# Moving the normed rows by 16 bytes relative to the streamed weights

## Chip, core and metric

The kernel runs on one core of one Trainium2 chip. The metric is the device time of one execution in microseconds, the median of several executions. TensorE (PE) multiplies, VectorE (DVE), ScalarE (ACT) and GpSimd (POOL) work elementwise, SyncE (SP) issues the weight transfers. PEld is the engine's load of stationary operands, which overlaps the matmul before.

## The reference

256 tokens (T) of width 1024 (D = 8 chunks of 128) pass through four layers in fp32. Two layers have a mixer, a memory cross attention and a product-key expert layer with 16384 experts; two have a mixer and a gated feed-forward layer of width 2816. Every sublayer begins with a norm and ends with an addition to h:

```python
def rmsnorm(x, g):
    y = x * lax.rsqrt(jnp.mean(x * x, axis=-1, keepdims=True) + EPS)
    return y * g

for l in range(DEPTH):                              # first block
    h = h + mixer[l](rmsnorm(h, mix_norm[l]))
    h = h + memory_cross_attn(rmsnorm(h, xattn_norm[l]), mem_n, ...)
    h = h + peer_ffn(rmsnorm(h, peer_norm[l]), ...) # gelu(x . u[e]) weights the rows v[e]
h = rmsnorm(h, final_norm)
for l in range(DEPTH):                              # second block
    h = h + mixer2[l](rmsnorm(h, attn_norm_2[l]))
    gate, up = split(rmsnorm(h, ffn_norm_2[l]) @ f_w_gate_up_2[l])
    h = h + (silu(gate) * up) @ f_w_down_2[l]
return rmsnorm(h, final_norm_2)
```

The expert layer multiplies the normed rows with all 16384 rows of peer_u and the weighted result with all of peer_v.

## The kernel before

Everything lies feature on partition: h and the normed rows are tiles of 128 partitions by 8 chunks by 256 tokens. Each fp32 number that enters a weight product is split into a high part, rounded to fp32r, and a low part, the rest: the normed rows into hnH and hnL, a weight block of 128x1024 into wH and wL. `product` makes one product out of three fp32r matmuls (L796 to L798 in the profile):

```python
pe.matmul(dst, lh, rh, start=start, stop=False, skip_group_check=True)  # weights high, rows high
pe.matmul(dst, lh, rl, start=False, stop=False, skip_group_check=True)  # weights high, rows low
pe.matmul(dst, ll, rh, start=False, stop=stop, skip_group_check=True)   # weights low, rows high
```

The second argument is the stationary operand (128x128, loaded ahead of its matmul), the third the moving one. The profile names the moving operand first: `bank<-hnH,wH` streams 256 columns of hnH past a 128x128 piece of wH.

The weights come as 864 blocks in the order of use, two at a time (1 MB) by SP (L660), into two ring slots. ACT copies a block to wH (L540), DVE or for some blocks POOL subtracts to wL (L551); there are four buffers of each. A buffer comes free when PE is done with its block.

The stages use `product` in these ways:

- `lin` (all linear layers, and `ffn` for gate and up): per output tile 8 chunks of 3 matmuls, the normed rows moving, 24 matmuls a block. `lin` also takes other moving tiles that are split in the same way: memH/memL, att_OTH/att_OTL, ycatH/ycatL, od_yH/od_yL, pr_hH/pr_hL, od_hH/od_hL, and ff_aH/ff_aL in the down layer.
- `acts` in `peer`: the same with a block of 128 experts, 128 blocks a layer. For 64 of them `tokens` follows each block with four 128x128 matmuls of one-hot rows (L1016).
- `outs` in `peer`: wH and wL are the moving operand (512 columns), wgtH/wgtL the stationary one, 12 matmuls a block.
- `token_major`: wH and wL moving (512 or 128 columns), memH or hnH stationary.

Every engine's instructions stand in the order in which the code is written; semaphores tie them together, and nothing is scheduled by the compiler.

Tiles are laid into the on-chip memory one behind the other in the order of their `sb` calls, and nothing else sets their addresses. Bytes from the start of a partition: arena 16512, ring 147584, wH 163968, wL 180352, the tile named shared (wgtH, wgtL) behind it, small 204928, snk, then hnH 205376 and hnL 213568, act_out 221760, vec, con 224352, iww, rb, slotT 226176. Modulo 256, wH and wL begin at 128 and hnH and hnL at 64: the rows begin 64 bytes below the weights. The other moving tiles of `lin` lie in the arena at the same remainder of 64 (gaps such as `od_gap` and `pr_gap` put them there); wgtH and wgtL have the weights' remainder of 128. All pieces that a weight product streams (1024 bytes of a chunk) or loads (512 bytes of a weight block) begin at those remainders; only in the few products of width 96, whose pieces have 384 bytes, every second one begins 128 bytes further.

Of the kernel before, what the change touches and what calls it, by code (L numbers as in the profile page):

```python
# [18 lines left out]
P = 128  # L19
T = 256  # L20
NT = T // P
D = 1024
DC = D // P
# [19 lines left out]
F32R = mybir.dt.float32r  # L43
# [272 lines left out]
def build_stacks(nc, x, mem, vecs, cst, w_stream, iw_w, sinks, rel_bias, c_cnt, c_neg, c_masks, c_bucket,  # L316
# [25 lines left out]
    with ExitStack() as ctx:  # L342
        def sb(name, shape, dt=F32):
            return ctx.enter_context(nc.sbuf_tensor(name, shape, dt))
# [4 lines left out]
        def stage(*wanted):  # L349

            with ExitStack() as scope:
                held = [scope.enter_context(nc.sbuf_tensor(name, [P] + list(shape), dt)) for name, shape, dt in wanted]
                return [t[tuple([slice(None)] * (len(w[1]) + 1))] for t, w in zip(held, wanted)]


        AR = 32768 - DC * T
        h = stage(("h_before", [AR], F32), ("h", [DC, T], F32))[1]
        (gates,) = stage(("gates", [N_KEYS, T], F32))
        h_back, sums = stage(("h_back", [DC, T], F32), ("sums", [NT, D], F32))

        MEM0, ATT0 = AR - 2 * DC * T - 16, AR - 2 * DC * T - 9344
        _, memH, memL = stage(("mem_before", [MEM0], F32), ("memH", [DC, T], F32R), ("memL", [DC, T], F32R))
# [68 lines left out]
        small = sb("small", [P, 96])  # L431
        snk = sb("snk", [P, 16])

        hnH, hnL = sb("hnH", [P, DC, T], F32R), sb("hnL", [P, DC, T], F32R)
        act_out = sb("act_out", [P, 2, T])
        root_sb, mem_root = act_out[:, 0, :], act_out[:, 1, :]
        vec = sb("vec", [P, NVEC])
        con = sb("con", [P, NCST])
        iww = sb("iww", [P, DC, 8])
        rb = sb("rb", [32, 8])  # L440
        slotT = sb("slotT", [P, 3, T])
        eps = small[:, 80:81]
        lbv = sb("lbv", [P, 24])
# [2160 lines left out]
```

## Time and profile before

| | us |
|---|---|
| median of 3 executions | 2812.21 (2805.3 to 2812.48) |
| profiled execution, its own time | 2813.5 |
| its span in the trace, first to last instruction | 2811.2 |
| PE busy | 2714.5 |
| DVE busy | 2053.1 |
| ACT busy | 1454.5 |
| mean granted TensorE clock | 0.99 |

The profiled execution stands 1.3 us above the median, and 2.3 us of it lie outside the span. A matmul's record overlaps that of its neighbours, since the ends are modelled; the time that one costs in a row of them is the distance between two starts. A row of the view by windows gives the matmuls that touch a stretch, the two or three that had begun before it among them.

### The profile page before, as it was taken

What the parts mean: (1) busy time and instruction counts of PE and PEld (TensorE: products, weight loads), DVE (VectorE), ACT (ScalarE), POOL (GpSimd) and SP (SyncE); (2) the same over time, 40 slices, a digit from 0 to 9 for tenths busy, and PEclk for the clock granted to TensorE, in tenths of its full rate; (3) what the DMA queues carried; (4) which work ended last, traced back from release to release, by engine and by line L of the source; (5) the groups of instructions that cost most, each with busy time, mean ns of one, the idle gap of its engine ahead of it and who ended that gap; (6) DMA issues with size and microseconds to landing.
All of it is one profiled execution on the core that took longest, in us unless ns stands there. A gap on an engine that the chain in (4) does not pass through costs nothing.

```text
span 2811.2 us, 57248 instructions
## 1 busy us (share of the span) xinstructions
PE 2714.5 (97%) x19552; PEld 2544.1 (90%) x19552; DVE 2053.1 (73%) x4430; ACT 1454.5 (52%) x2378; POOL 177.8 (6%) x141
## 2 busy tenths in 40 slices
PE   7999999999999999989999999999999989999998
PEld 6999899999988888979998999988888889999998
DVE  8557997886566667876699888567776877666665
ACT  5455345444555555555544444455555565446544
POOL 0004000000000000000374000000000100000000
PEclk9999999999999999999999999999999999999999
DMA  5445566455766665424456555676666525563454
GB/s 190 176 157 184 204 215 213 174 182 195 261 242 242 242 242 179 149 78 165 165 182 217 191 172 183 218 258 242 242 242 242 187 81 182 190 230 117 177 184 178
DMA packets 140451, 546.19 MB, mean 194 GB/s; under 512 B 15784, under 2 KB 81592, under 8 KB 83616
## 3 DMA queue, kind: packets, MB, share of 16 engines
q1 hardware_dynamic: 63216, 455.38, 44.8%
q10 hardware_dynamic: 73728, 67.14, 7.4%
q0 software_dynamic: 3376, 21.88, 2.0%
q8 instruction: 87, 1.43, 0.2%
q14 instruction: 44, 0.36, 0.0%
HBM read 505.53 MB, written 40.91 MB: 194 GB/s over the span
## 4 chain that ended last, share of the span: by engine, by line
PE 78%; DVE 15%; DMA 2%; ACT 2%; issue 2%; DVEq 0%; ACTq 0%; SPq 0%
PE bank L796 23%; PE bank L797 23%; PE bank L798 23%; PE bank L1016 4%; DVE wL L551 4%; DMA ring<-in_w_stream 2%; PE bank L917 1%; ACT wH L540 1%; PE bank L937 1%; DVE pr_eq L1969 1%; DVE pr_eq L1971 1%; DVE pr_m L1973 1%; PE bank L928 1%; DVE pr_m L1924 0%; DVE pr_i L1924 0%
## 5 line engine op out<-in xcount | busy, mean ns | idle before, releaser
L551 DVE TENSOR_TENSOR wL<-ring,wH 128x1024 fp32r<-128x1024 f32 x809 | 988.1, 1224 | 605.5 <-ACT wH L540 602.5
L540 ACT ACTIVATE wH<-ring 128x1024 fp32r<-128x1024 f32 x864 | 907.3, 1055 | 423.2 <-DMA ring<-in_w_stream 252.6
L796 PE MATMUL bank<-hnH,wH 128*128 128x256 f32 x3528 | 1003.3, 284 | 34.5 <-DVE wL L551 26.6
L797 PE MATMUL bank<-hnL,wH 128*128 128x256 f32 x3528 | 984.0, 279 | 0.0
L798 PE MATMUL bank<-hnH,wL 128*128 128x256 f32 x3528 | 983.5, 279 | 0.0
L796 PEld LDWEIGHTS bank<-hnH,wH 128*128 128x128 f32 x3528 | 667.5, 189 | 45.7 <-issue 22.9
L797 PEld LDWEIGHTS bank<-hnL,wH 128*128 128x128 f32 x3528 | 667.2, 189 | 0.5 <-issue 0.2
L798 PEld LDWEIGHTS bank<-hnH,wL 128*128 128x128 f32 x3528 | 665.1, 189 | 0.0
L796 PE MATMUL bank<-wH,wgtH 128*128 128x512 f32 x1024 | 398.5, 389 | 0.3 <-DVE wgtL L2010 0.3
L798 PE MATMUL bank<-wH,wgtL 128*128 128x512 f32 x1024 | 398.4, 389 | 0.0
L797 PE MATMUL bank<-wL,wgtH 128*128 128x512 f32 x1024 | 398.3, 389 | 0.0
L1478 ACT ACTIVATE act_out<-bank 128x256 f32<-128x256 f32 x256 | 97.6, 381 | 339.0 <-PE bank L798 280.1
L1502 ACT ACTIVATE wgtH<-gates 128x256 fp32r (+1 forms) x256 | 106.9, 418 | 252.1 <-PE bank L798 251.9
L796 PEld LDWEIGHTS bank<-wH,wgtH 128*128 128x128 f32 x1024 | 192.2, 188 | 40.6 <-issue 0.7
L798 PEld LDWEIGHTS bank<-wH,wgtL 128*128 128x128 f32 x1024 | 192.2, 188 | 39.9
L797 PEld LDWEIGHTS bank<-wL,wgtH 128*128 128x128 f32 x1024 | 192.2, 188 | 39.7
L1997 DVE TENSOR_SCALAR onehot<-con,slotT 128x128 f32<-128x128 f32 x512 | 174.1, 340 | 0.0
L551 POOL TENSOR_TENSOR wL<-ring,wH 128x1024 fp32r<-128x1024 f32 x55 | 141.8, 2598 | 68.9 <-DVE wL L551 41.2
L1996 DVE TENSOR_SCALAR onehot<-con,slotT 128x128 f32<-128x128 f32 x512 | 143.1, 280 | 0.0
L1016 PE MATMUL bank<-onehot 128*128 128x128 f32 x1024 | 134.9, 274 | 0.0
L1016 PEld LDWEIGHTS bank<-onehot 128*128 128x128 f32 x1024 | 124.8, 191 | 0.0
L2010 DVE TENSOR_TENSOR wgtL<-gates,wgtH 128x256 fp32r<-128x256 f32 x256 | 107.6, 420 | 8.8 <-ACT wgtH L1502 8.4
(411 smaller groups left out, 3535.3 us busy)
## 6 DMA issues: line engine op xcount, KB each, us to landing
ring<-in_w_stream SPq DMA_DIRECT2D x432, 1024.0 KB, 4.9
act_parked<-act_out ACTq DMA_DIRECT2D x256, 128.0 KB, 3.0
act_in<-act_parked ACTq DMA_DIRECT2D x256, 128.0 KB, 2.7
sw_bias<-in_c_swa POOLq DMA_DIRECT2D x1, 4096.0 KB, 15.7
relb_rows<-rel_table POOLq DMA_DIRECT2D x1, 2048.0 KB, 10.0
h_parked<-h POOLq DMA_DIRECT2D x2, 1024.0 KB, 6.3
h_back<-h_parked POOLq DMA_DIRECT2D x2, 1024.0 KB, 6.2
od_relb<-relb_rows POOLq DMA_DIRECT2D x2, 1024.0 KB, 7.4
```

What stands on the lines that cost most here:

```text
L540: eng.activation(wH[:, b % NBUF, :], raw(b), ACT.Copy).then_inc(w_high, 1)
L551: eng.tensor_tensor(wL[:, b % NBUF, :], raw(b), wH[:, b % NBUF, :].bitcast(F32), ALU.subtract).then_inc(w_low, 1)
L796: pe.matmul(dst, lh, rh, start=start, stop=False, skip_group_check=True)
L797: pe.matmul(dst, lh, rl, start=False, stop=False, skip_group_check=True)
L798: return pe.matmul(dst, ll, rh, start=False, stop=stop, skip_group_check=True)
L917: last = pe.matmul(ps[:, 0:span], qs[c][:, tt * P:(tt + 1) * P], ks[c][:, 0:span], start=(c == 0), stop=(c == len(qs) - 1))
L1016: last = pe.matmul(psacc[j][:, m * P:(m + 1) * P], onehot[:, k, :], onehot[:, 8 + k, :], start=True, stop=True)
L1478: act.activation(act_out[:, c % 2, :], psum[c % BANKS][:, 0:T], ACT.Gelu_apprx_tanh).then_inc(u_read, 1)
L1502: act.activation(wgtH[:, c % 2, :].unsqueeze(1), gates[:, bass.ds(i * 4 + c, 1), :], ACT.Copy).then_inc(wgt_high, 1)
L1996: dve.tensor_scalar(onehot[:, k, :], iota, slotT[:, 2, bass.ds(tok, 1)], None, ALU.is_equal)
L1997: last = dve.tensor_scalar(onehot[:, 8 + k, :], iota, slotT[:, 1, bass.ds(tok, 1)], slotT[:, 0, bass.ds(tok, 1)], ALU.is_equal, ALU.mult)
L2010: dve.tensor_tensor(wgtL[:, c % 2, :].unsqueeze(1), gates[:, bass.ds(i * 4 + c, 1), :], wgtH[:, c % 2, :].bitcast(F32).unsqueeze(1), ALU.s ...
```

## The change

The two tiles hnH and hnL (8192 bytes each) become views into one tile hn_both of 4104 fp32r elements, from its element 4 on. Both halves thus begin 16 bytes later, 205392 and 213584: remainder 80 modulo 256, 48 bytes below the weight tiles. The tile is 32 bytes longer than the two were, so act_out, vec, con, iww move up by 32 bytes (con to 224384, remainder 128). The table rb (32 partitions by 8, the position bias table, read by one matmul at the start) goes into columns 16 to 23 of small, which nothing else uses, and its 32 bytes drop out, so that slotT and what follows stay where they were.

```diff
+        def pair(tile, first, chunks):
+
+            return [tile[:, first + s * chunks * 256:first + (s + 1) * chunks * 256].rearrange(
+                "p (a b) -> p a b", a=chunks) for s in range(2)]
+
...
-        hnH, hnL = sb("hnH", [P, DC, T], F32R), sb("hnL", [P, DC, T], F32R)
+        hnH, hnL = pair(sb("hn_both", [P, 16 * 256 + 8], F32R), 4, DC)
...
-        rb = sb("rb", [32, 8])
+        rb = small[0:32, 16:24]
```

With the names hnH, hnL and hn_both taken as one, and rb and small, the instructions of PE, DVE, ACT, POOL and SP stand in the same order before and after, one for one, with the same shapes. What differs is the addresses in them.

## Rows read from the trace of the kernel before

**Rows 1.** The page: busy time, and the chain that ended last.
```profile
PE 2714.5 (97%) x19552; PEld 2544.1 (90%) x19552; DVE 2053.1 (73%) x4430; ACT 1454.5 (52%) x2378; POOL 177.8 (6%) x141
...
PE 78%; DVE 15%; DMA 2%; ACT 2%; issue 2%; DVEq 0%; ACTq 0%; SPq 0%
PE bank L796 23%; PE bank L797 23%; PE bank L798 23%; PE bank L1016 4%; DVE wL L551 4%; DMA ring<-in_w_stream 2%; PE bank L917 1%; ACT wH L540 1%; PE bank L937 1%; DVE pr_eq L1969 1%; DVE pr_eq L1971 1%; DVE pr_m L1973 1%; PE bank L928 1%; DVE pr_m L1924 0%; DVE pr_i L1924 0%
```

**Rows 2.** Longest wait of PE: line, waited for, us in total, times, longest.
```profile
PE bank L796 <- DVE wL L551: 43.7, 37, 7.2
```

**Rows 3.** PE by windows: stretch, length, busy (matmuls), clock, DMA share, GB/s.
```profile
315.00:340.00 25.00, 24.02 (x175) 1.00 0.63 216
...
450.00:670.00 220.00, 220.00 (x1918) 1.00 0.51 179
690.00:740.00 50.00, 50.00 (x443) 1.00 0.73 242
800.00:1000.00 200.00, 200.00 (x884) 1.00 0.68 242
...
1550.00:1770.00 220.00, 220.00 (x1917) 1.00 0.52 181
2345.00:2455.00 110.00, 110.00 (x936) 1.00 0.52 190
...
2622.00:2655.00 33.00, 33.00 (x282) 1.00 0.55 192
```

**Rows 4.** Timeline of PE, `acts` without one-hot: start us, us, instruction; 21 steps.
```profile
699.91 0.28 PE L797 MATMUL bank<-hnL,wH 128*128 128x256 f32 x1
...
702.29 0.28 PE L797 MATMUL bank<-hnL,wH 128*128 128x256 f32 x1
```

**Rows 5.** The same, gate and up layer; 20 steps.
```profile
2399.78 0.28 PE L796 MATMUL bank<-hnH,wH 128*128 128x256 f32 x1
...
2402.14 0.28 PE L798 MATMUL bank<-hnH,wL 128*128 128x256 f32 x1
```

**Rows 6.** Line L797: count, duration ns min/median/max, first and last start.
```profile
L797 PE MATMUL bank<-hnL,wH x3528: 276/276/420, 13.8 to 2734.2; 128*128 128x256 f32 x195, 128*96 128x256 f32 x1
...
L797 PE MATMUL bank<-wL,wgtH x1024: 387/389/395, 744.6 to 2191.8; 128*128 128x512 f32 x171
...
L797 PE MATMUL bank<-ff_aL,wH x352: 281/281/420, 2456.1 to 2800.1; 128*128 128x256 f32 x176
...
L797 PE MATMUL bank<-wL,memH x64: 388/392/398, 126.9 to 320.8; 128*128 128x512 f32 x64
...
L797 PE MATMUL bank<-od_yL,wH x64: 276/276/276, 1266.5 to 1287.9; 128*128 128x256 f32 x64
```

**Rows 7.** Timeline of PE, blocks of `acts` with one-hot matmuls between.
```profile
475.89 1.05 PE L1016 MATMUL bank<-onehot 128*128 128x128 f32 x8
476.70 0.36 PE L796 MATMUL bank<-hnH,wH 128*128 128x256 f32 x1
476.90 0.28 PE L797 MATMUL bank<-hnL,wH 128*128 128x256 f32 x1
...
479.61 1.06 PE L1016 MATMUL bank<-onehot 128*128 128x128 f32 x8
...
483.24 1.05 PE L1016 MATMUL bank<-onehot 128*128 128x128 f32 x8
```

**Rows 8.** The page, DMA issues: line, count, KB each, us to landing.
```profile
act_parked<-act_out ACTq DMA_DIRECT2D x256, 128.0 KB, 3.0
```

**Rows 9.** The page's groups: the transposes of the attention.
```profile
L928 PE MATMUL bank<-con,att_P 128*128 128x128 f32 x152 | 33.3, 280 | 2.6 <-ACT att_P L1410 2.2
```

**Rows 10.** Timeline of PE, gate and up layer: two restarts behind a wait.
```profile
2661.32 0.36 PE L796 MATMUL bank<-hnH,wH 128*128 128x256 f32 x1
...
2666.89 0.36 PE L796 MATMUL bank<-hnH,wH 128*128 128x256 f32 x1
```

**Rows 11.** Timeline of PE: eight transposes in a row and what follows.
```profile
2574.21 1.04 PE L907 MATMUL bank<-con,att_O 128*128 128x128 f32 x8
2575.09 0.28 PE L917 MATMUL bank<-sw_k,sw_q 128*128 128x128 f32 x1
```

## The prediction, made before the changed kernel ran

> **What bounds the kernel now.** I read the page first: PE is busy for 2714.5 of 2811.2 us, the chain of work that ended last runs through PE for 78% of the span, and 69% of the span are the three lines of `product` [rows 1]. The waits say how little PE is held up: the longest group is 43.7 us in 37 waits for the low parts of the weights [rows 2]. So nearly everywhere the time of a stage is the number of its matmuls times their distance.
>
> Is that distance the same everywhere? The windows tell: in 690 to 740 us, pure `acts`, 443 matmuls touch 50 us; less the three that had begun before, that is 50/440 = 113.6 ns each. In 2345 to 2455 us, gate and up, the same instruction with the same 256 columns takes 110/933 = 117.9 ns, at the same granted clock of 1.00 [rows 3]. No wait stands between the matmuls of either stretch. The timeline confirms it: 21 steps in 2.38 us, 113.3 ns each [rows 4], and 20 steps in 2.36 us, 118.0 each [rows 5]; over long stretches the second is 117.8. Call them the **short and the long step**, 4.45 ns apart. I sorted all 10,584 matmuls with 256 columns of normed rows by the distance to the next start, at 116 ns: 5697 are followed by a short step, 4548 by a long one, and 339 by something else (restarts behind a wait or another kind of matmul); of each kind two examples stand in the rows. The durations carry the same mark, 276 ns with the short step and 281 with the long: the rows of od_yL stay at 276 from first to last, and those of ff_aL, median 281, are nearly all long [rows 6].
>
> A step, once taken, is kept: in 2622 to 2655 us the long one runs without a short one between [rows 3]. It changes after a restart. Behind the one-hot matmuls a block begins with a step of 200 ns (476.70 to 476.90), then either stays long, and has taken 3.72 us from one-hot to one-hot (475.89 to 479.61), or drops to short after two or three steps and takes 3.63 us (479.61 to 483.24) [rows 7]. Here the two kinds alternate. That looks like two streams that lock to each other: the load of the next stationary piece (512 bytes) runs while 1024 bytes of rows are streamed. What the shift can change is this lock.
>
> **The change part by part.** No instruction is added, removed or moved on any engine, no wait and no transfer either. Only addresses differ.
>
> (1) The one matmul that reads the bias table and its small transfer get another address. It happens once; I take 0.
>
> (2) act_out moves by 32 bytes. The 256 transfers from it land after 3.0 us [rows 8], act_out has two halves that alternate, and ACT is busy for 52% of the span [rows 1]. A landing slower by a tenth (0.3 us) hides. 0.
>
> (3) con moves by 32 bytes, to the weights' own remainder. It is the moving operand of the transposes, 152 of them in the attention [rows 9] and 124 elsewhere. Should each of these 276 take the step difference of 4.45 ns more or less, that is 1.2 us either way. 0, bound 1.2 us.
>
> (4) The normed rows as the moving operand: 10,584 matmuls. Bounds: if every long step becomes short, 4548 x 4.45 = 20.2 us are won on PE; if every short one becomes long, 5697 x 4.45 = 25.4 us are lost. The trace has no row of normed rows at another remainder, so the nearest rows must do. They are the 512-column matmuls, in which rows and weights change places. With wgtH stationary, at the weights' own remainder, durations are 387/389/395 ns (min, median, max); with memH stationary, 64 bytes below, 388/392/398 [rows 6]. Shape and engine are the same, and the one whose operands lie at different remainders is longer by 3 ns in the median. In 800 to 1000 us the first kind keeps 200/881 = 227 ns throughout [rows 3], twice the short step, while the second's starts are 226 to 232 ns apart in the timeline, with the same mark in the durations. So the distance of the two operands modulo 256 does bear on how the loads and the stream get in each other's way, by an amount of the size of our 4.45 ns; and a distance at which the long step is absent exists, in that shape. Which way 16 bytes go, the rows don't say. I take the side on which the lock comes undone, because the short step looks like the floor: no stretch of 256 columns has a steadier step below it, and 227 ns for 512 columns is the same rate. A placement that breaks the lock leads to the floor, while one that keeps it leads to about today's mix.
>
> What of the 20.2 us is on the path:
> - In the one-hot stretches a block takes (220 us)/(1915/32) = 3.68 us in both layers [rows 3]. All short it would be 0.81 us of one-hot, a first step of 0.20 and 23 x 0.1133 = 3.62 us. 128 blocks x 0.06 = 7.7 us. PE waits for nothing here.
> - In gate and up 1650 of the long steps lie, 933 of them in 2345 to 2455 and 279 in 2622 to 2655 [rows 3]. Where this layer runs at the short step, PE catches up with the weights: it restarts once every 48 matmuls, at 2661.32 and 2666.89, 5.57 us apart [rows 10], where 48 long steps are 5.65. So only 0.08 us per 48 are won: 34 x 0.08 = 2.7 us instead of 7.3.
> - The other long steps of the normed rows, 4548 - 1685 (one-hot) - 1650 = 1213, lie in the linear layers and in the first blocks of `acts`; 315 to 340 us is all long but for what is not of normed rows [rows 3]. 1213 x 4.45 = 5.4 us.
>
> (5) The other moving tiles (att_OTH, ff_aH, pr_hH and so on) stay 64 bytes below. 1724 of their matmuls take long steps, 1035 in the down layer [rows 6]. They may inherit the short step where hn hands it on without a restart: at most 1724 x 4.45 = 7.7 us more. Each of these stages begins with a wait, so I take 0 and keep the 7.7 for the lower end.
>
> Sum: 7.7 + 2.7 + 5.4 = 15.8 us. The profiled execution's 2813.5 becomes 2797.7; it stands 1.3 us above the median, so the median becomes **2796**.
>
> A rule that speaks against any effect is in the Trainium skill, "SBUF — State Buffer", section "Who interferes with whom": PE has one read port for the moving operand and an independent one for the weight load, and never waits on anyone. By that rule the two streams could not lock, and the change would give 2812, the time of the first rival below. The two steps of one instruction at one clock [rows 4, 5] don't fit it, but they don't show that the address is what matters.
>
> **The rivals.**
>
> *The mix stays.* The step may be chosen at a restart by when it falls, not by the address: both steps occur at the same distance of addresses today, and blocks alternate without any address changing but the buffer's. Then the long share stays near 4548 of 10,245, and redrawing it by a tenth moves 1000 x 4.45 = 4.5 us. Time 2808 to 2817, middle 2812. It would also be the time if loads and stream had nothing to do with each other. For it: the alternation [rows 7]. Against: the 512-column rows [rows 6].
>
> *The long step becomes the rule* (the slower side). The place is the same, the step of the normed rows: 16 bytes closer, the load and the stream may meet sooner after the start of a matmul, and the drop after two or three long steps [rows 7] no longer happens. Price: 5697 x 4.45 = 25.4 us, less about 1 us where PE would have waited for the weights anyway: 2836. It decides from 8.4 us on, when 1900 of today's 5697 short steps turn long. A third and worse step is possible too and would end higher. For it: gate and up is today locked to the long step for 800 matmuls in a row, so it is the more stable of the two. Against: every long stretch but those in gate, up and down ends at a restart.
>
> *A step below the short one.* Eight fp32 transposes of 128 columns take 0.88 us, 110 ns each [rows 11], and in long rows of them the timeline has 109 between two starts, against 113 for 256 fp32r columns. If the new distance took the rows there, 10,245 matmuls would save about 4 ns more each, half of it hidden behind waits for weights: 2796 - 20 = 2776. Nothing in the trace shows fp32r rows at that pace. The Trainium skill has a figure near it: "TensorE: Matmul & The Clock Gate", section "Back-to-back issue gap", gives 262 cycles for 256 columns, which as an estimate is 109 ns at 2.4 GHz.
>
> **How the numbers follow.** Long steps gone from the normed rows: 0.42, 2796 (own range 2786 to 2803, the upper end if a third of them stay). Mix stays: 0.27. More long steps: 0.25, 2836 at the full price, 2822 at half. Below the short step: 0.06. A difference of 0.3%, 8.4 us, is about what can be told from no change here. Faster takes the first and last: 0.48. Same 0.27, slower 0.25. The range leaves out most of the rival below the floor and the worst part of the slower one: 2784 to 2832.
>
> **What the profile of the changed kernel would show.** The rows of 690 to 740 should stay at 113 ns, those of 2345 to 2455 fall to 116 or less (5.57 us per 48) with waits for wL appearing, and every one-hot block should take 3.62 us, so the whole stretch of 64 blocks 232 instead of 236 us. The median duration of the hn matmuls stays 276 and their mean falls; outs keeps 227 ns. If the one-hot blocks still alternate between 3.63 and 3.72 us, the address doesn't matter and the mix rival holds. If `acts` in 690 to 740 is at 118 ns, the slower rival holds. I would be wrong in kind, not in size, if DVE, ACT or a transfer changed its duration with these addresses.

## The result, and the profile after

The changed kernel takes 2830.62 us (median of 5 executions, 2826.2 to 2838.8), the kernel before 2812.3 (5 executions, 2805.3 to 2813.9): ratio 1.0077, 95% interval 1.0057 to 1.0096. (The ratio with its interval is an estimate of its own and not the quotient of these two medians, which is 1.0065: the loss is 18 us by the medians and 22 by the ratio.) It is slower, inside the range, on the other side of the forecast. Its profiled execution took 2826.2 us, span 2823.9, at a mean clock of 0.994, and is the fastest of the five.

PE by windows in the changed kernel, the same stretches as in [rows 3]; columns: stretch, length, busy (matmuls), clock, DMA share, GB/s.

```profile
450.00:670.00 220.00, 220.00 (x1878) 1.00 0.51 177
690.00:740.00 50.00, 50.00 (x422) 1.00 0.68 222
800.00:1000.00 200.00, 200.00 (x884) 1.00 0.68 242
1550.00:1770.00 220.00, 220.00 (x1878) 1.00 0.52 178
2345.00:2455.00 110.00, 110.00 (x922) 1.00 0.50 174
2622.00:2655.00 33.00, 33.00 (x276) 1.00 0.45 160
```

In 690 to 740 us, where the short step of 113.3 ns ruled, 50/419 = 119.3 ns pass between two matmuls. In 450 to 670 a block with its one-hot matmuls takes 220/(1875/32) = 3.75 us instead of 3.68. `outs`, which has no normed rows, keeps its 884 matmuls in 200 us.

The timeline of PE (start us, us, instruction) shows how. This is gate and up, where [rows 5] had nothing but long steps:

```profile
2400.28 0.28 PE L802 MATMUL bank<-hn_both,wH 128*128 128x256 f32 x1
2400.39 0.28 PE L803 MATMUL bank<-hn_both,wL 128*128 128x256 f32 x1
2400.51 0.28 PE L801 MATMUL bank<-hn_both,wH 128*128 128x256 f32 x1
2400.63 0.28 PE L802 MATMUL bank<-hn_both,wH 128*128 128x256 f32 x1
2400.75 0.28 PE L803 MATMUL bank<-hn_both,wL 128*128 128x256 f32 x1
2400.87 0.29 PE L801 MATMUL bank<-hn_both,wH 128*128 128x256 f32 x1
2400.99 0.28 PE L802 MATMUL bank<-hn_both,wH 128*128 128x256 f32 x1
2401.11 0.28 PE L803 MATMUL bank<-hn_both,wL 128*128 128x256 f32 x1
2401.23 0.28 PE L801 MATMUL bank<-hn_both,wH 128*128 128x256 f32 x1
```

Neither of the two steps holds. The nine rows span a group of eight steps, to the nanosecond 115, 119, 118, 118, 120, 124, 121, 119, which then begins anew: 119.2 on average. Sorted as before, 1348 matmuls of the normed rows are followed by a step of up to 115 ns, 6696 by one of 116 to 120 and 2540 by something else, mostly 121 to 125: near 1 to 5 to 2, the shares of that group, over the whole kernel.

I sorted the starts of both traces again, steps in a row (below 130 ns) apart from those that hold a restart or a wait, and measured the stages between the first and last one-hot, `outs` and down matmuls:

| | before | after |
|---|---|---|
| normed rows, 256 columns: steps in a row | 10,280, 115.36 ns, 1185.9 us | 10,281, 119.08 ns, 1224.3 us |
| the same: restarts and waits | 101.8 us | 91.2 us |
| other moving tiles, 256 columns: in a row | 115.90 ns, 350.1 us | 114.58 ns, 349.7 us |
| the same: restarts and waits | 43.6 us | 32.1 us |
| stage of `acts` with one-hot, each layer | 232.5 | 237.2 |
| `acts` after it, each layer | 65.4 | 68.8 |
| `outs` | 347.9 and 348.5 | 347.9 and 349.8 |
| down layers | 64.2 and 65.8 | 61.3 and 64.0 |

(The mean granted clock of the two profiled executions is 0.990 and 0.994. That is not what made restarts and waits smaller: e2_rows_alone below, with the rows at the same place and a clock of 0.990, has 92.5 and 35.6 us of them.) The steps alone cost 38.4 us more. In `acts` from the first one-hot block on, where PE waits for nothing, 2 x (4.7 + 3.4) = 16.2 us of it are in the time. Of the other 22.2 us nothing is left in these two traces, whose spans differ by 12.7 us; restarts and waits are 22.1 us less. Two lines say from where. The waits of PE (line, waited for, us, times, longest) shrank from 43.7 us [rows 2]:

```profile
PE bank L801 <- DVE wL L556: 30.1, 32, 5.1
```

And the down layers, whose tiles did not move, lost part of the long steps that filled them before: durations (ns min/median/max) of its low rows, 281 in the median in [rows 6].

```profile
L802 PE MATMUL bank<-ff_aL,wH x352: 276/276/281, 2471.8 to 2812.8; 128*128 128x256 f32 x176
```

Before, all 1036 of their steps in a row are long. Now both layers reach the short step four steps after the last normed row; the first keeps it, the second turns long again behind a restart, for 460 of its 528 matmuls.

### The profile page after: what moved, and what is told of

It reads as the page before. It is cut to its first block, busy times and chain, and to the rows that moved or that the text cites. A ratio compares the mean times of both kernels' runs of the same rounds, so it can differ in the third digit from the quotient of the medians.

```text
span 2823.9 us, 57248 instructions
## 1 busy us (share of the span) xinstructions
PE 2740.1 (97%) x19552; PEld 2569.7 (91%) x19552; DVE 2048.9 (73%) x4430; ACT 1456.8 (52%) x2378; POOL 180.3 (6%) x141
## 4 chain that ended last, share of the span: by engine, by line
PE 74%; DVE 14%; DMA 4%; ACT 3%; issue 3%; POOL 2%; SPq 0%; DVEq 0%; ACTq 0%
PE bank L801 22%; PE bank L803 21%; PE bank L802 21%; DVE wL L556 4%; PE bank L1021 4%; DMA ring<-in_w_stream 3%; ACT wH L545 2%; POOL wL L556 2%; PE bank L922 1%; PE bank L942 1%; DMA act_parked<-act_out 1%; PE bank L933 1%; DVE pr_m L1978 0%; DVE pr_eq L1976 0%; DVE pr_i L1929 0%
## 5 line engine op out<-in xcount | busy, mean ns | idle before, releaser
L801 PE MATMUL bank<-hn_both,wH 128*128 128x256 f32 x3528 | 1016.9, 288 | 25.3 <-DVE wL L556 16.2
L802 PE MATMUL bank<-hn_both,wH 128*128 128x256 f32 x3528 | 999.7, 283 | 0.0
L803 PE MATMUL bank<-hn_both,wL 128*128 128x256 f32 x3528 | 999.4, 283 | 0.0
L801 PEld LDWEIGHTS bank<-hn_both,wH 128*128 128x128 f32 x3528 | 670.2, 190 | 35.4 <-issue 16.7
L802 PEld LDWEIGHTS bank<-hn_both,wH 128*128 128x128 f32 x3528 | 670.6, 190 | 0.5 <-issue 0.2
L803 PEld LDWEIGHTS bank<-hn_both,wL 128*128 128x128 f32 x3528 | 670.0, 190 | 0.0
## 6 DMA issues: line engine op xcount, KB each, us to landing
relb_rows<-rel_table POOLq DMA_DIRECT2D x1, 2048.0 KB, 11.5
```

Of the source, the lines that this page charges most:

```text
L803: return pe.matmul(dst, ll, rh, start=False, stop=stop, skip_group_check=True)
```

## Is it the distance, and of what?

Theory A: the address of the normed rows relative to the weights sets the steps. Its rivals: the loss comes from the neighbours that moved along (con, act_out), or the longer steps are made by other engines' or transfers' accesses. The page of the changed kernel gave the first rival a footing, since the landing of act_parked had gone from 3.0 us [rows 8] to 3.5:

```profile
act_parked<-act_out ACTq DMA_DIRECT2D x256, 128.0 KB, 3.5
```

**The two halves of the change apart.** e1_rows_back takes the changed kernel and puts the rows back, everything else moved:

```diff
-        hnH, hnL = pair(sb("hn_both", [P, 16 * 256 + 8], F32R), 4, DC)
+        hnH, hnL = pair(sb("hn_both", [P, 16 * 256 + 8], F32R), 0, DC)
```

> The changed kernel with the rows back at the tile's start, 64 bytes below the weights, while act_out, vec, con and iww stay 32 bytes higher and the bias table stays in small. Theory A (rows' distance): 2812, ratio 1.000 to the kernel before, steps of 113.3 and 117.8 ns. Rival C (moved neighbours, the landing of act_out that went from 3.0 to 3.5 us among them): 2830.

Measured: 2811.92 us, ratio 1.0001 (0.998 to 1.0022). The mean step of the normed rows is 115.5 ns, and act_parked lands after 3.0 us again although act_out has the changed kernel's address. So the 3.5 isn't made by that address; what made it is not shown.

e2_rows_alone takes the kernel before and moves the rows alone. Small and snk are cut up into the gaps around them:

```diff
-        small = sb("small", [P, 96])
-        snk = sb("snk", [P, 16])
+        low_part = sb("small_low", [P, 48])
...
-        hnH, hnL = sb("hnH", [P, DC, T], F32R), sb("hnL", [P, DC, T], F32R)
+        hn_both = sb("hn_both", [P, 16 * 256 + 8], F32R)
+        hnH, hnL = [hn_both[:, 4 + i * 2048:4 + (i + 1) * 2048].rearrange("p (a b) -> p a b", a=DC) for i in range(2)]
+        snk, high_part = sb("snk", [P, 16]), sb("small_high", [P, 40])
```

> The kernel before with the normed rows alone 48 bytes below the weights: act_out, vec, con, iww, the bias table and everything above keep their addresses; small and snk are cut up into the space around the rows. Theory A: 2830, ratio 1.006 to 1.010, the step pattern with mean 119.4 ns. Rival C: 2812.

Measured: 2828.26 us, ratio 1.0064 (1.0046 to 1.0082), mean step 119.06 ns. Its windows (columns as above) repeat those of the changed kernel:

```profile
450.00:670.00 220.00, 220.00 (x1878) 1.00 0.51 178
690.00:740.00 50.00, 50.00 (x422) 1.00 0.65 223
```

Here act_parked lands after 2.9 us, so the loss comes without the slower landing too. The loss is the rows' place, and the bias table, act_out, vec, con and iww cost nothing that these runs can tell (the interval of e1_rows_back is 6 us either way).

**PE alone.** m1_scan leaves the model out, keeps the tiles' addresses, takes real weights, with x in the place of the normed rows, and lets PE run the three matmuls over 16 starts of the rows (this and the next four programs ran once each):

```diff
+            for start in STARTS:
+                hot()
+                for b in range(5):
+                    block_of(start, b)
+                for b in range(3):
+                    hot()
+                    last = block_of(start, b)
```

(`block_of` is `product` over 8 chunks, `hot` eight small fp32 matmuls in the place of the one-hot ones.)

> This kernel leaves the whole model out and only writes x back. PE alone works: once two weight blocks pairs and the rows are in place, the three fp32r matmuls of product run over 16 starts of the rows, 0 to 240 bytes above the weights modulo 256 in steps of 16, for each start 8 small fp32 matmuls, 5 blocks of 24 matmuls in a row, then 3 blocks with 8 small ones ahead of each. ACT, DVE and the queues are idle meanwhile, and the tiles lie at the addresses of the full kernel. Theory A, the distance of the rows' and the weights' addresses sets the step: at 192 (64 below) steps of 113.3 or 117.8 ns, at 208 (48 below) a pattern with mean 119.4 ns in every block, other means elsewhere. Rival B, other engines or transfers reading nearby cause the long steps: 113.3 ns at every start. Rival C, the neighbours that moved (con, act_out) cause the loss: no difference between 192 and 208.

Its page says who is at work (engines, and ACT's busy tenths in 40 slices of the span):

```profile
PE 478.7 (96%) x4096; PEld 478.5 (96%) x4096; DVE 5.3 (1%) x5; ACT 10.9 (2%) x8; POOL 0.2 (0%) x4
...
ACT  6200000000000000000000000000000000000000
```

and the windows (columns as above) of the placements 192, 208, 96 and 112 bytes above the weights, 10 us of blocks in a row each, two matmuls of each count having begun before:

```profile
382.00:392.00 10.00, 10.00 (x90) 1.00 0.01 2
410.00:420.00 10.00, 10.00 (x86) 1.00 0.01 2
202.00:212.00 10.00, 10.00 (x85) 1.00 0.01 2
232.00:242.00 10.00, 10.00 (x90) 1.00 0.01 2
```

| bytes above the weights mod 256 | ns a step, blocks in a row | ns a step, three blocks behind small matmuls |
|---|---|---|
| 0 | 119.9 | 119.6, 119.6, 119.6 |
| 16 | 118.7 | 116.8, 116.7, 116.7 |
| 32 | 116.7 | 116.5, 117.9, 116.5 |
| 48, 64, 80 | 118.3, 117.8, 118.3 | 118.3, 117.8, 118.6 to 120.1 |
| 96 | 119.95 | 120.1, 119.7, 119.7 |
| **112** | **113.7** | 115.8, 115.7, 115.8 |
| 128, 144, 160 | 118.7, 118.7, 118.7 | 118.6 to 120.0, 116.6 to 118.9, 117.5 to 118.6 |
| 176 | 119.2 | 118.8, 118.8, 118.8 |
| **192** (before) | **113.5** | 117.8, 113.9, 117.8 |
| **208** (the change) | **119.1** | 119.0, 119.0, 119.0 |
| 224 | 118.4 | 118.3, 118.7, 118.3 |
| 240 | 117.2 | 117.2, 117.4, 117.3 |

With ACT, DVE and the queues at rest the bare PE shows all that the full kernel shows: at 192 both steps, and one block at 117.8, the next at 113.9, in turn, as in [rows 7]; at 208 the broken pattern at 119.1 in every block. Rivals B and C fall. And the short step is no floor that one drops to when a lock breaks. It belongs to 2 of 16 places. (The 115.8 at 112 is a mean over a run-in: behind small matmuls a block takes ten steps of about 118.7 ns and then stays at 113.3. At 192 the blocks that become short do so after about five steps.)

**Distance or remainder.** In all kernels so far the weights begin at remainder 128, so a distance to them and a remainder of the rows' own can't be told apart. m2_weights_up moves the weights up by 16 bytes and leaves the rows' starts:

```diff
-        WPAD = 0
+        WPAD = 4
```

> As m1_scan (the model left out), but the weights begin 16 bytes higher, while the rows start at the same 16 addresses. Theory A in the form distance alone: each start behaves as the start 16 bytes lower did in m1_scan, so the 113.3/117.8 pattern is at the rows' start 208 and the 119.4 pattern at 224. Rival A2, the rows' own remainder modulo 64 or 256 alone: each start behaves as in m1_scan, 119.4 at 208. Rival A3, the weights' own remainder matters too: a third picture.

The 113.3 ns moved along: they are at the rows' start 208, which is again 192 above the weights (blocks in a row 113.5, behind small ones 115.0), and no longer at start 192 (118.8). But the second good place is gone: 112 above the weights gives 120.0 (start 128), and so do the distances 128 and 144. (The 115.0 is a run-in of about eight steps, then 113.3: all three blocks become short here, none stays long as at 192 in m1_scan.) The windows of starts 208 and 128:

```profile
412.00:422.00 10.00, 10.00 (x91) 1.00 0.01 2
262.00:272.00 10.00, 10.00 (x85) 1.00 0.01 2
```

Set side by side by distance (ns a step, blocks in a row), the two scans differ at most places:

| bytes above the weights mod 256 | 0 | 32 | 80 | 96 | 112 | 128 | 192 | 208 |
|---|---|---|---|---|---|---|---|---|
| m1_scan, weights at 128 | 119.9 | 116.7 | 118.3 | 119.95 | 113.7 | 118.7 | 113.5 | 119.1 |
| m2_weights_up, weights at 144 | 116.7 | 118.3 | 118.2 | 120.0 | 120.0 | 120.0 | 113.5 | 117.8 |

Only 80, 96 and 192 of the 16 distances repeat to 0.2 ns; by the rows' own start the short step doesn't repeat either (192 becomes 118.8). So neither distance nor remainder decides alone: a third picture, as in A3, in which the places of both tiles matter, with 192 good in both. The table of m1_scan is one for weights that begin at 128, as in every full kernel here.

**Finer, and the low rows apart.** m3_fine:

```diff
-                hi, lo = [rows[:, start + s * 2048:start + (s + 1) * 2048] for s in range(2)]
+                high, low, cols, span = start
+                hi, lo = rows[:, high:high + 2048], rows[:, low + 2048:low + 4096]
```

> The model left out, PE alone, as in m1_scan; 24 placements, each with 4 blocks of 24 in a row and 6 blocks behind small matmuls: distances of 180 to 204 and 104 to 120 bytes above the weights in steps of 4, the distances 192 and 112 once more with the rows 256 bytes lower, and the high rows at 192 with the low rows at 0, 32, 64, 96, 112, 128, 160, 176, 208, 240. Theory A (the distance modulo 256 between load and stream): 192 settles on 113.3 ns again, with the rows 256 bytes lower too; the 4-byte neighbours of 192 differ from it by less than the 16-byte neighbours do, between 113.3 and 119; with low rows elsewhere the mean lies between 113.3 and 119. Rival, only whole lines of 16 bytes count: 192 and 196 to 204 alike.

Measured means, blocks in a row: 180: 123.3 (steps of 121 to 125; 120.1 to 120.4 behind small ones), 184: 120.0, 188: 118.6, **192: 113.4**, 196: 121.6, 200: 120.0, 204: 117.8; 104: 120.2, 108: 119.9, **112: 113.8**, 116: 121.8, 120: 122.1. With the rows 256 bytes lower, 192 and 112 repeat to 0.02 ns. I had expected the neighbours at 4 bytes to be milder than those at 16. Above the good places they are among the worst of all. The good place is gone 4 bytes to either side, so it is no matter of 16-byte lines either. The windows at 192 and 196:

```profile
147.00:156.00 9.00, 9.00 (x82) 1.00 0.01 2
188.00:197.00 9.00, 9.00 (x76) 1.00 0.01 2
```

With the high rows at 192 and the low rows elsewhere, only 176 and 240 came below 117 (115.8 and 116.6 in a row); the other eight gave 117.1 to 120.0. Both must be in place.

**Shorter loads, longer streams.** m4_mixed varies the columns of the stationary piece and of the stream (the edit is shown against m1_scan):

```diff
-                    W, L = wH[:, b % 4, k * P:(k + 1) * P], wL[:, b % 4, k * P:(k + 1) * P]
+                    W, L = wH[:, b % 4, k * P:k * P + cols], wL[:, b % 4, k * P:k * P + cols]
```

> The model left out, PE alone. Low rows at 192 with the high rows at ten other distances, high at 112 with the low at five; stationary pieces of 64 and 96 columns at 192, 208, 96 and 0; and 512 moving columns at those four. Theory A's mechanism, the load of the next piece gets in the way of the stream: with pieces of 64 columns, a load of half the length, the step is 113.3 ns at every distance, the 117 to 120 of 128 columns gone, and with 96 columns it lies between; 512 moving columns cost 226.7 ns plus at most what one load costs (4 to 7 ns), at all four distances. Rival, the stream alone is slower where its rows begin badly: 64 columns at 208, 96 and 0 stay at 119 to 120 ns, and 512 columns take 238 to 240.

| distance | 64 columns loaded | 96 | 128 (m1_scan) | 128, 512 streamed |
|---|---|---|---|---|
| 192 | 119.0 | 116.7 | 113.5 | 233.4 |
| 208 | 116.6 | 118.8 | 119.1 | 234.6 |
| 96 | 116.6 | 117.8 | 119.95 | 233.5 |
| 0 | 113.5 | 116.0 | 119.9 | 227.0 |

Both expectations for the short load missed: the long steps did not vanish with half the load, and didn't stay either. They moved. With 64 columns 0 is the good place and 192, the best for 128 columns, the worst. The rows and their place are the same along each line of the first three columns, and only the load differs (and with it how many partitions are written), so the step is made by load and stream together. With 512 columns 0 is the best of the four as well, 227.0 against 233.4 at 192. That agrees with the 227 ns of wgtH in `outs`, where both tiles have one remainder [rows 3]. For memH [rows 6] there is no counterpart: its stream begins 64 bytes above the loaded piece, and the scan has 64 below. The bad places cost 6.7 to 8 ns more than 226.7, the expectation said at most 4 to 7.

Other pairs of places for high and low rows (high at ten distances with the low at 192, high at 112 with the low at five) gave 117.5 to 121.4 ns, none as good as 192 or 112 for both.

**One load, one stream.** m5_orders has one product in all places, other orders of the three, and a fixed stationary piece:

```diff
+                    for n, pair in enumerate(order.split()):
+                        last = pe.matmul(ps, piece[pair[0]], moving[pair[1]], ...)
```

> The model left out, PE alone. Three things. First one product only, high weights with high rows, in all places, at 16 distances: if the step is a matter of one load against one stream, each distance has one steady step, with 113.3 ns at 192 and 112 and 117 to 120 elsewhere, as in m1_scan; if the three tiles of a product must fit together, the curve is another. Second, other orders of the three matmuls (low weights second, or low rows first) at six distances: since all four tiles lie at equal remainders, a theory of the distance alone expects the same means as in m1_scan to 0.5 ns; a theory of history (which load meets which stream, and where the last one ended) expects others. Third, the same stationary piece in all 24 matmuls of a block: distance modulo 256 alone says as before (113.4 or 117.8 at 192, 119.1 at 208, 119.9 at 96).

With high weights by high rows alone, all 16 places give the means in a row of the table above, at most 0.3 ns apart (192: 113.6 in a row, then 117.8, 113.95, 117.8; 208: 119.0; 96: 119.9). Other orders: the same within 0.3 ns, and a piece that never changes too (192: 113.4, 208: 119.1, 96: 120.0). So which tiles meet, and which chunk, doesn't matter; their places modulo 256 do. One case differs, and it tells what a lock is: at 192 in the order WR, WH, LH the 72 matmuls in a row ran at 117.8 throughout instead of 113.5. The blocks behind small matmuls show a rule in it. At 192, with the weights at 128, long and short alternate without exception, in m1_scan, m3_fine and here, and this row follows a block with the short step at the same place, so it was the turn of the long one. In the kernel before, the one-hot blocks of each layer alternate as strictly. So at that place there are two steady steps, and something that the block before leaves behind picks one at each restart; what it is, is not shown. At 208 there is one pattern. (Other places have two as well: behind small matmuls 32 gives 116.5 or 117.9 and 144 gives 118.9 or 116.6.)

The windows for 192 in the order of the kernel (high weights only), and in the one that fell into the long step:

```profile
370.00:378.00 8.00, 8.00 (x74) 1.00 0.01 2
...
512.00:520.00 8.00, 8.00 (x71) 1.00 0.01 2
```

## What a nanosecond of the step is worth

Three more full kernels move the rows alone, as e2_rows_alone does, with another start. e3_rows_96 (96 bytes above), e4_rows_112 and e5_rows_32 differ from it in these numbers, and in which columns of small go where:

```diff
-        low_part = sb("small_low", [P, 48])
+        low_part = sb("small_low", [P, 24])
...
-        snk, high_part = sb("snk", [P, 16]), sb("small_high", [P, 40])
+        snk, high_part = sb("snk", [P, 16]), sb("small_high", [P, 64])
```

That is e4. In e3 the rows also begin with the first element of hn_both instead of the fifth, and in e5 as well, behind 8 columns of small.

> The kernel before with the normed rows alone moved to 96 bytes above the weights modulo 256, the worst distance of the bare scan (119.9 ns against 119.1 at 208). Theory A: steps of 119.9 ns in the whole kernel, time 2828 to 2840, ratio 1.007 to 1.011, not below the kernel with 48 bytes below. Rival, the bare scan doesn't carry over: some other time, near 2810.

> The kernel before with the normed rows alone 112 bytes above the weights, the one other distance that settled on 113.3 ns in the bare scan. Theory A: long stretches at 113.3 ns, one-hot blocks near 115.8 ns a step (3.68 us a block), gate and up limited by the weights, time 2798 to 2812, ratio 0.995 to 1.000. Rival, 64 below is alone in that and the first scan was chance: 2825 or more.

> The kernel before with the normed rows alone 32 bytes above the weights modulo 256, where the bare scan gives 116.8 ns a step, between today's mix (115.4 over the whole kernel) and 119.1 at 48 below. Theory A with the waits counted: the steps in a row of the normed rows cost 10,280 x (116.8 - 115.4) = 14 to 15 us more, and about half of it is taken back from waits for weights, as in the changed kernel (38.4 us more of steps, 18 us more of time): 2816 to 2822, ratio 1.002 to 1.004. Rival, nothing is taken back and the changed kernel lost time by steps that the median doesn't show: 2826 or more. Rival, every distance but 192 and 112 locks to the same loss: 2828.

| rows above the weights | mean step in a row, ns | steps against before, us | median, ratio (95%) |
|---|---|---|---|
| 192 (before) | 115.4 | | 2812.3 |
| 112, e4 | 114.5 | -9 | 2810.47, 0.9995 (0.9981 to 1.0009) |
| 32, e5 | 117.0 | +17 | 2821.7, 1.0039 (1.0025 to 1.0053) |
| 208, the change | 119.1 | +38 | 2830.62, 1.0077 (1.0057 to 1.0096) |
| 208, e2 | 119.1 | +38 | 2828.26, 1.0064 (1.0046 to 1.0082) |
| 96, e3 | 119.9 | +46 | 2838.2, 1.0105 (1.0066 to 1.0144) |

(Steps against before: the mean difference times 10,280.) The bare scan orders the full kernels rightly, and of each microsecond of steps about a half to two thirds reaches the end: 11 of 17, 18 to 22 of 38, 30 of 46. The rival "every other distance locks to the same loss" falls with e5's step of 117.0 ns. "Nothing is taken back" would make e5's 17 us a ratio of 1.0060, just outside its interval, and the changed kernel's 38 us one of 1.0137, far outside.

e4 is the test of my own forecast, for in it the long steps are largely gone. Its windows:

```profile
450.00:670.00 220.00, 220.00 (x1919) 1.00 0.52 182
690.00:740.00 50.00, 50.00 (x444) 1.00 0.72 242
...
2345.00:2455.00 110.00, 109.69 (x949) 1.00 0.55 192
2622.00:2655.00 33.00, 33.00 (x289) 1.00 0.55 191
```

In 2345 to 2455 us 949 matmuls stand where 936 did [rows 3], and the kernel is no faster by a measurable amount. The one-hot blocks still take 3.67 us. At 192 every second block is long to its end; at 112 each block begins with ten steps of about 118.7 ns and then takes twelve of 113.3. The starts of one such block, its first and second matmul, the one ten steps on, and its last:

```profile
478.05 0.37 PE L807 MATMUL bank<-hn_both,wH 128*128 128x256 f32 x1
478.26 0.28 PE L808 MATMUL bank<-hn_both,wH 128*128 128x256 f32 x1
...
479.44 0.28 PE L809 MATMUL bank<-hn_both,wL 128*128 128x256 f32 x1
...
480.81 0.28 PE L809 MATMUL bank<-hn_both,wL 128*128 128x256 f32 x1
```

The stage up to the second down layer won 2.4 us, the two down layers gave back 2.2 and 0.6 (66.4 us each). Restarts and waits of the normed rows rose from 101.8 to 121.4 us, and the waits of PE for the low weights are nearly what they were [rows 2]:

```profile
PE bank L807 <- DVE wL L562: 40.5, 35, 6.2
```

No placement that I tried beats the kernel before clearly; e4 equals it.

## Why the prediction was wrong, point by point

- **What bounds the kernel, and the two steps**: right. PE's distance between matmuls sets the expert layers, both steps are there in the bare PE, and the start after a restart picks between them. That load and stream lock to each other was an inference. m4_mixed shows that the load is part of it, m5_orders that the same tiles at the same place can take either step.
- **Parts 1 to 3 at nothing**: right, within what e1_rows_back can tell (0.998 to 1.0022). The landing of 3.5 us in the changed kernel wasn't the doing of act_out's address.
- **Part 4, the sign: the step that failed.** I wrote that a placement that breaks the lock leads to the floor, "because the short step looks like the floor". The rows said only that no steadier step lay below 113.3 ns. They didn't say what a kernel without a lock does. It falls into patterns of 116.7 to 119.9 ns on average at the other 16-byte places, and up to 123.3 between them. The short step is itself a lock, held at two places of sixteen, and gone 4 bytes to either side. The lock came undone indeed, and that was the loss: 119.08 ns against 115.36.
- **The 512-column rows** were read rightly in kind, for the distance does bear on the step (227.0 at 0, 233.4 at 192 in m4_mixed). What they could not show is which distance is good for another length of stream: at 256 columns 0 gives 119.9 and 192 gives 113.5, the reverse. I used rows of another shape to choose a side. I also took the distance without its sign: the stream begins 64 bytes above the loaded piece in the memH rows, and 64 below in the normed rows.
- **The bounds of part 4** were too narrow upwards. They assumed that a step is one of the two seen, at most 25.4 us of loss; the steps cost 38.4.
- **What is on the path**: for gate and up I counted 2.7 of 7.3 us, a share of about 0.4, and for everything else 1. In `acts` from the one-hot blocks on 1 is right (4.7 + 3.4 us a layer, all in the time). In the first blocks of `acts` and the linear layers, which I also took at 1, it isn't: the 984 matmuls of 321 to 446 us lose 3.3 us in steps and take only 1.3 us longer. Over all stages but those of 16.2 us nothing is left in the two traces, and 2 us by the medians. e4_rows_112 shows what a gain would have met: 9 us fewer in steps, 1 us in the median (interval 5 us less to 3 more). Even with the lock undone to the good side my 15.8 us would not have come whole.
- **Part 5**: the other tiles did take the short step more often in the changed kernel (median of ff_aL 276, mean of all 114.58 instead of 115.90 ns), for another reason than I gave: the normed rows did not hand on a short step, they no longer handed on the long one. The down layer begins with steps of 121, 114, 123, 119 ns and then 113, where before it went on with 118 from gate and up. Their time in a row fell by 0.4 us only, as more of their matmuls run in a row, and their restarts and waits by 11.5.
- **The rival that came nearest** is the slower one, right in sign and in place, and with 2836 against 2831 near in size. Its mechanism did not happen: the long step of 117.8 ns did not become the rule, a pattern without either step did. That the size fits is luck, for two errors met in it: a worse step than it priced (it named one in passing), and more taken back by waits than the 1 us that it allowed. That the time lies inside the range is owed to this rival, not to the forecast. **The mix stays** was wrong: the start picks only where the address offers two steps, and at 208 it offers one pattern, worse than both. The pace below the short step appeared nowhere.
- The rule of the Trainium skill that spoke against any effect ("SBUF — State Buffer", "Who interferes with whom": the moving operand and the weight load have independent ports, and PE never waits) fits the part that says other engines don't matter: m1_scan has ACT at rest and the same steps. Between load and stream it doesn't hold as a rule on time: 113.3 to 123.3 ns by nothing but their places. Whether a port is the reason, no run shows.

What stays open is the mechanism below that: why 192 and 112 are good for a load of 128 columns, and 0 for one of 64 or a stream of 512, why 112 is no longer good when both tiles lie 16 bytes higher while 192 is, and what makes the blocks at 192 alternate. Nor was it tried whether another way into a block (the small matmuls ahead of it) would make the start pick the short step at 192 each time, or what the full kernel takes with weights and rows both 16 bytes higher, where in m2_weights_up every block became short.

## What to carry to other kernels

When PE is the bound, take the distance between two starts of one instruction in each stretch, and compare stretches: two values at one clock and without a wait are a finding, and a bare PE program with the kernel's own addresses, loads and streams gives a table of 16 placements in half a millisecond of chip time. Scan it with the weights at their own address, for the exact number of columns loaded and streamed, in steps of one element, and with restarts in it, before an address is changed in the kernel; what is good for one shape is bad for another. A state that looks like the floor may be the fragile one, and leaving a lock is as likely to lose as to win.

## What the runs showed of the hardware that I had not expected

- One fp32r matmul of 256 columns takes between 113.3 and 123.3 ns by where its rows and the pieces loaded begin modulo 256, with every other engine at rest; one element (4 bytes) makes the difference between the best (113.4 at 192) and one of the worst (121.6 at 196).
- The pattern depends on the loaded columns: at 192, 128 columns 113.5 ns, 96 columns 116.7, 64 columns 119.0. A shorter load can be slower.
- A steady step survives hundreds of matmuls: 1024 long ones in a row from gate and up into the down layer of the kernel before, and 72 at 117.8 in m5_orders with the same tiles and distance that otherwise ran at 113.5.
- At 192, with the weights at 128, blocks behind small matmuls take the two steps in strict turn, in three bare programs and in the one-hot blocks of both layers of the kernel before.
